# A step list for each engine in the banded mixer, two score buffers in turn, and merged up-products in the perceptrons of a six-layer transformer on one Trainium2 core

## The reference, cut to what matters

```python
def swa_sink_attention(h, w_in, b_in, sinks, w_out, cos, sin):   # 16 query heads, 2 key heads, head size 64
    qkv = h @ w_in + b_in
    q, k, v = jnp.split(qkv, [SWA_HEADS * D, (SWA_HEADS + KV) * D], axis=-1)
    q = apply_partial_rope(q.reshape(B, S, SWA_HEADS, D), cos, sin) * (D ** -0.5)
    k = apply_partial_rope(k.reshape(B, S, KV, D), cos, sin)
    ...
    s = jnp.where(mask, s, -jnp.inf)              # window of 128 keys back, causal
    m = jnp.maximum(jnp.max(s, axis=-1, keepdims=True), sink)
    e = jnp.exp(s - m)
    p = e / (jnp.sum(e, axis=-1, keepdims=True) + jnp.exp(sink - m))
    return (p @ v2).reshape(B, S, SWA_HEADS * D) @ w_out

def sqrelu_mlp(h, w_up, w_down):                  # 1024 -> 4096 -> 1024
    a = jnp.maximum(h @ w_up, 0)
    return (a * a) @ w_down
```

## Time and profile before

| | |
|---|---|
| runs (3) | 1585.6, 1586.77, 1589.15 us; median 1586.77 |
| profiled execution | 1580.09 us, span 1578.1 us, mean granted TensorE clock 0.974 |
| TensorE busy | 1483.8 us, 94% of the span |
| VectorE, ScalarE busy | 935.8 us (59%), 807.1 us (51%) |
| DMA | 242.24 MB, mean 153 GB/s |
| chain that ended last | TensorE 82%, ScalarE 8%, VectorE 6%, DMA 3% |

### The profile page before, as it was taken

The page is one execution under the profiler, slowest core; times in us unless marked ns, Lnnn a source line. Parts: engine busy times, 40 slices in busy tenths (PEclk is TensorE's granted clock), DMA queues, the critical chain, the costliest instruction groups (busy, mean ns, idle before and its releaser), DMA issues.

```text
span 1578.1 us, 20946 instructions
## 1 busy us (share of the span) xinstructions
PE 1483.8 (94%) x8815; PEld 1291.9 (82%) x8815; DVE 935.8 (59%) x1292; ACT 807.1 (51%) x1251; POOL 39.3 (2%) x72
## 2 busy tenths in 40 slices
PE   7988999999999999888999999989999899889988
PEld 5777999978889998766899987768999778777877
DVE  6673555465745455555455456645455479868984
ACT  6584444454534344433444436765344357756783
POOL 3000000000000000000000000000000010101010
PEclk8999999999999999999999999989999989989998
DMA  8432454544235454511354556324454534425430
GB/s 281 157 110 107 166 208 172 202 160 161 107 116 204 170 203 151 196 54 54 117 204 177 197 175 203 122 101 161 166 208 172 201 103 161 146 81 164 166 108 27
DMA packets 119465, 242.24 MB, mean 153 GB/s; under 512 B 3042, under 2 KB 48908, under 8 KB 119372
## 3 DMA queue, kind: packets, MB, share of 16 engines
q1 hardware_dynamic: 117616, 237.25, 42.5%
q0 software_dynamic: 1408, 3.52, 1.0%
q10 hardware_dynamic: 348, 0.13, 0.0%
HBM read 239.84 MB, written 1.05 MB: 153 GB/s over the span
## 4 chain that ended last, share of the span: by engine, by line
PE 82%; ACT 8%; DVE 6%; DMA 3%; issue 1%; POOL 0%; SPq 0%; DVEq 0%; POOLq 0%; ACTq 0%
PE pair L1092 24%; PE pair L1094 24%; PE pair L1093 23%; PE pair L1295 3%; PE pair L1246 2%; PE pair L1186 2%; DVE wlo L1553 2%; ACT sm L762 1%; ACT whi L656 1%; PE pair L1272 1%; ACT xhi L688 1%; PE pair L1241 1%; DVE xlo L1590 1%; DMA raw<-in_diff_w_out 1%; DMA raw<-in_w_in 1%
## 5 line engine op out<-in xcount | busy, mean ns | idle before, releaser
L1553 DVE TENSOR_TENSOR wlo<-raw,whi 128x2048 fp32r<-128x2048 f32 (+2 forms) x240 | 504.9, 2141 | 76.1 <-ACT whi L656 74.2
L656 ACT ACTIVATE whi<-raw 128x2048 fp32r<-128x2048 f32 (+2 forms) x240 | 416.5, 1782 | 103.8 <-DMA raw<-in_mlp_w_down 46.3
L1092 PE MATMUL pair<-xhi,whi 128*128 128x256 f32 x1024 | 291.0, 284 | 6.9 <-DVE xlo L1590 6.9
L1094 PE MATMUL pair<-xhi,wlo 128*128 128x256 f32 x1024 | 289.7, 283 | 0.0
L1093 PE MATMUL pair<-xlo,whi 128*128 128x256 f32 x1024 | 289.7, 283 | 0.0
L1092 PE MATMUL pair<-whi,xhi 128*128 128x512 f32 (+2 forms) x656 | 261.6, 399 | 22.7 <-DVE wlo L1553 13.3
L1094 PE MATMUL pair<-whi,xlo 128*128 128x512 f32 (+2 forms) x656 | 253.1, 386 | 0.0
L1093 PE MATMUL pair<-wlo,xhi 128*128 128x512 f32 (+2 forms) x656 | 252.8, 385 | 0.0
L1092 PE MATMUL pair<-whi,ahi 128*128 128x512 f32 x608 | 242.0, 398 | 5.6 <-DVE alo L1590 5.6
L1093 PE MATMUL pair<-wlo,ahi 128*128 128x512 f32 x608 | 239.1, 393 | 0.0
L1094 PE MATMUL pair<-whi,alo 128*128 128x512 f32 x608 | 238.9, 393 | 0.0
(11 more groups left out here) (248 smaller groups left out, 1465.5 us busy)
## 6 DMA issues: line engine op xcount, KB each, us to landing
raw<-in_mlp_w_up SPq DMA_DIRECT2D x32, 2048.0 KB, 8.6
raw<-in_mlp_w_down SPq DMA_DIRECT2D x32, 2048.0 KB, 7.5
raw<-in_diff_w_in SPq DMA_DIRECT2D x22, 1024.0 KB, 7.2
raw<-in_w_in SPq DMA_DIRECT2D x10, 2048.0 KB, 8.1
raw<-in_moba_w_in SPq DMA_DIRECT2D x12, 1024.0 KB, 6.2
raw<-in_diff_w_out SPq DMA_DIRECT2D x4, 2048.0 KB, 7.9
raw<-in_w_uq SPq DMA_DIRECT2D x4, 1152.0 KB, 5.4
raw<-in_moba_w_out SPq DMA_DIRECT2D x2, 2048.0 KB, 8.3
```

The source lines that it names most:

```text
L656: act.activation(whi[:, s, cols], raw[:, s, cols], ACT.Copy).then_inc(*t["hi_split"].one())
L1092: pe.matmul(dst, x_hi, w_hi, start=first, stop=False)
L1094: return pe.matmul(dst, x_lo, w_hi, start=False, stop=last)
L1553: dve.tensor_tensor(wlo[:, s, cols], raw[:, s, cols], whi[:, s, cols].bitcast(FP32), ALU.subtract)\
```

## The change

1. The banded mixer gets a list for each engine (`swa_tensor_steps`, `swa_scalar_steps`, `swa_vector_steps`) and its own reader `mix_swa` on each engine, with `BankUses` over `swa_bank_uses`. Head pairs use PSUM pair 0 and pair 3 in turn (`score_pair`). The first input block is queries 0 to 511, then keys and values, then the other queries. Queries are transposed for two head pairs at a time, into four half-pairs. The copy to `pT` moves from VectorE to ScalarE. The outputs' features go to `ahi_tiles` and `alo_tiles` instead of `xhi` and `xlo`. The first output block takes its units by columns, the second by features.
2. `keep_busy` is removed.
3. `xhi` and `xlo` are neighbours in one tile, `xparts`. A unit of an up block becomes one matmul of 512 columns (weights hi by both parts of x) and one of 256 (weights lo by x hi), so 64 matmuls a block instead of 96. Each bank holds one hidden tile: 256 columns of the large sum and 256 of the small. An up block uses both pairs 0 and 1. In each half ScalarE copies the small sums, VectorE adds the large ones from PSUM and frees the pair, VectorE takes relu times itself in one operation, ScalarE rounds, VectorE subtracts. A half starts when its two hidden tiles are done, the first one in the middle of the block.

```diff
+def swa_bank_uses():
+    scores = [[f"{what}{hp}" for hp in range(j, HEAD_PAIRS, 2) for what in ("scores", "turn")] for j in range(2)]
+    uses = {2: ["in2"], 3: ["in1"] + scores[1], 0: scores[0], 6: ["heads2"], 7: ["heads3"], 8: ["keys0"]}
+    for j in range(2):
+        uses[4 + j] = [f"heads{j}"] + [f"{what}{q}" for q in (j, 2 + j) for what in ("outputs", "features")]
+    return uses
...
-        xhi = sb("xhi", [P, KT, SEQ], FP32R)
-        xlo = sb("xlo", [P, KT, SEQ], FP32R)
+        xparts = sb("xparts", [P, 2, KT, SEQ], FP32R)
+        xhi, xlo = xparts[:, 0, :, :], xparts[:, 1, :, :]
...
-                return [(1024, 256), (0, BANK), (BANK, BANK)]
+                return [(0, BANK), (1024, 256), (BANK, BANK)]
...
+            steps = part("in", 0, 0, 8) + part("in", 1, 0, 7) + [("heads", 0)] + part("in", 1, 7, 8) + [("heads", 1)]
+            steps += part("in", 2, 0, 3) + [("keys", 0)] + part("in", 2, 3, 5) + [("scores", 0), ("scores", 1)]
+            steps += part("in", 2, 5, 8) + [("turn", 0), ("turn", 1), ("scores", 2), ("mix", 0), ("scores", 3), ("heads", 2)]
+            steps += [("heads", 3), ("mix", 1), ("turn", 2), ("features", 0), ("turn", 3), ("scores", 4)]
+            steps += [("mix", 2), ("scores", 5), ("mix", 3), ("turn", 4), ("features", 1), ("turn", 5)]
+            steps += [("scores", 6), ("mix", 4), ("scores", 7)] + part("out", 0, 0, 3) + [("mix", 5), ("turn", 7), ("turn", 6)]
+            steps += part("out", 0, 3, 4) + [("features", 2), ("mix", 6), ("mix", 7)] + part("out", 0, 4, 7) + [("features", 3)]
+            steps += part("out", 0, 7, 8) + part("out", 1, 0, 8)
...
+            steps = [("in_results", 0), ("in_results", 1), ("in_results", 2), ("split", 0), ("split", 1), ("heads", 0)]
+            steps += [("heads", 1), ("split", 0), ("split", 1), ("keys", 0), ("split", 0), ("split", 1)]
+            steps += [("scores", 0), ("scores", 1), ("outputs", 0), ("turn", 0), ("turn", 1), ("scores", 2)]
...
+            steps = [("split", 0), ("split", 1), ("in_results", 0), ("rope", 0), ("in_results", 1), ("heads", 0)]
+            steps += [("heads", 1), ("rope", 1), ("split", 0), ("keys", 0), ("split", 1), ("scores", 0)]
+            steps += [("scores", 1), ("split", 0), ("in_results", 2), ("rope", 2), ("scores", 2), ("scores", 3)]
...
-            return 0
+            return 3 * (hp % 2) if mixer == "swa" else 0
...
-                    used()
-                    act.activation(relu_at[b], pair[b][:, :, :].rearrange("p b n -> p (b n)"), ACT.Relu)\
-                        .then_inc(*t.emptied[b].one())
-                    act.wait_ge(*t.emptied[b].now())
-                    act.activation(ahi[:, b, :, :].rearrange("p f n -> p (f n)"), relu_at[b], ACT.Square)\
-                        .then_inc(*t["ahi_written"].one())
+                    for part in range(2):
+                        used(1)
+                        act.activation(rising(part), pair[part][:, :, SEQ:2 * SEQ], ACT.Copy).then_inc(*t["small_copied"].one())
+                        t.emptied[part].n += 1
+                    for part in range(2):
+                        act.wait_ge(*t["squared"].after())
+                        act.activation(risen_to(ahi, j % 2, part), risen(part), ACT.Copy).then_inc(*t["ahi_written"].one())
...
-                    free(j % 2)
...
-                        m = products(pair_tile(j % 2, f), (w_hi[:, k, cols], w_lo[:, k, cols]),
-                                     (xhi[:, k, :], xlo[:, k, :]), k == 0, k == KT - 1)
-                        if f % 2 and k == KT - 1:
+                        if k == 0 and f // 2 == 0:
+                            free(f % 2)
+                        cols, sums = slice(f * P, (f + 1) * P), pair[f % 2][:, f // 2, :]
+                        pe.matmul(sums, w_hi[:, k, cols], xparts[:, :, k, :], start=k == 0, stop=False)
+                        m = pe.matmul(sums[:, 0:SEQ], w_lo[:, k, cols], xhi[:, k, :], start=False, stop=k == KT - 1)
+                        if f // 2 and k == KT - 1:
...
+                    for part in range(2):
+                        used(1)
+                        dve.wait_ge(*t["small_copied"].after())
+                        dve.tensor_tensor(rising(part), pair[part][:, :, 0:SEQ], rising(part), ALU.add)\
+                            .then_inc(*t.emptied[part].one())
+                        dve.wait_ge(*t.emptied[part].now())
+                        dve.scalar_tensor_tensor(out=risen(part), in0=rising(part), scalar=0.0, in1=rising(part), op0=ALU.max,
+                                                 op1=ALU.mult).then_inc(*t["squared"].one())
+                    for part in range(2):
+                        dve.wait_ge(*t["squared"].now(1 - part))
+                        dve.wait_ge(*t["ahi_written"].after())
+                        dve.tensor_tensor(risen_to(alo, j % 2, part), risen(part), risen_to(ahi, j % 2, part).bitcast(FP32),
+                                          ALU.subtract).then_inc(*t["alo_written"].one())
```

More of the change, by code:

```diff
@@ new lines, in swa_tensor_steps, with part @@
+        def swa_tensor_steps():
+            def part(what, b, first, last):
+                return [(what, b, e) for e in range(first, last)]
+            steps = part("in", 0, 0, 8) + part("in", 1, 0, 7) + [("heads", 0)] + part("in", 1, 7, 8) + [("heads", 1)]
[6 more added lines that the diff above has]
+            steps += part("out", 0, 7, 8) + part("out", 1, 0, 8)
+            return steps
@@ L1633, in norm @@
                     split()
-            def biased_results(n):
-                c0, w = in_blocks("swa")[n]
-                p = 2 + n % 2
-                for tt in range(TT):
-                    used(1)
-                    m = dve.scalar_tensor_tensor(out=qkv[:, tt, c0:c0 + w], in0=pair[p][:, tt, 0:w], scalar=rstd[:, tt:tt + 1],
-                                                 in1=swab[:, c0:c0 + w], op0=ALU.mult, op1=ALU.add)
-                m.then_inc(*t.emptied[p].one())
             def rope(view, n, half, tables, place):
@@ L1822, in mix_tokens, with biased_results, rotated_keys @@
                         split((n,))
+            def biased_results(n, done):
+                c0, w = in_blocks("swa")[n]
+                for tt in range(TT):
+                    used(1)
+                    m = dve.scalar_tensor_tensor(out=qkv[:, tt, c0:c0 + w], in0=pair[2 + n % 2][:, tt, 0:w],
+                                                 scalar=rstd[:, tt:tt + 1], in1=swab[:, c0:c0 + w], op0=ALU.mult, op1=ALU.add)
+                m.then_inc(*done)
+            def rotated_keys():
+                chain(rotate_heads(D, 2))
+                k = qkv[:, :, 1024:1152].rearrange("p t (g d) -> p t g d", g=2)
+                both = qkv[:, :, 1280:1536].rearrange("p t (g r d) -> p t g r d", g=2, r=2)
+                for r in range(2):
+                    m = dve.tensor_copy(both[:, :, :, r, :], k)
+                return m
```

245 lines of the change are left out of this document (172 added, 73 removed).

## The result

| | before | after |
|---|---|---|
| median of the runs | 1587.96 us (1585.6 to 1591.03, 4 runs) | 1539.4 us (1537.26 to 1541.15, 4 runs) |
| ratio after / before | | 0.9686, 95% interval 0.9664 to 0.9707 |
| span, granted clock | 1578.1 us, 0.974 | 1539.4 us, 0.974 |

The change is 3% faster; 1544 was forecast. The page of the changed kernel, part 1 (beside the earlier trace rows): TensorE has 1088 instructions fewer and is busy 22.6 us less, though the span is 38.7 us shorter. The other 16.1 us were idle time. VectorE's busy time grew by 44.0 us, where about 40 were forecast.

What follows compares the result with a forecast made beforehand. TensorE, busy 94% of the span, bounds the kernel; the banded mixer has slack. Merge 13.5 plus mixer 29 is 42.5 us off 1580.1, giving 1537.6, with 6.7 us for the median 1544; forecast 1538 to 1550, range 1532 to 1560.

Steps and rivals of the forecast that it cites:

- the 79.2 us of work: Banded mixer, first input product to closing residual transposes: TensorE's summed work after the change at full clock, against 118.4 us before.
- 3 for handovers: Banded mixer: some 0.1 us for each handover that the listed durations leave out, 3 us added in all.
- The wait at heads 0: Banded mixer, before the first queries' transposes: TensorE newly waits 2.5 us for VectorE's split, bias and turning.
- the idle time in the attention: Banded mixer's attention without filler until scores 7: idle bits of 0.4 to 1.0 us, together 4 us.
- the walk: Banded mixer: the four lists stepped through with the durations, giving 7 us idle and about 4 us a pair.
- The tight place (3): Banded mixer: ScalarE's output-block splits precede the first exponentials, which end at 674; TensorE is covered until 674.4, under 1 us.
- my three conditions for being wrong: Merged matmul over 0.235 us, TensorE idle in the perceptrons, or granted clock below 0.8 in the attention stretch.
- my upper bound: Perceptron up blocks: a merged product at twice the pace of 256 columns, 0.2398 us, where nothing is gained.
- Rival 3: Perceptrons: merge fails, by two chunks at two matmuls' pace or the page's 2.5 ns; 11 to 13.5 us less, chance 0.07.
- cover: Perceptrons: time between wlo being ready and the next up block that reads it, 2.2 us before, 1.4 after.
- rival 4: Perceptrons: the split of the block after next makes TensorE wait; 4 us more gives 73 us lost, 1617; chance 0.02.
- that offset: Whole kernel: the median of the runs lies 6.7 us above the profiled execution, added to 1537.6 to expect 1544.

Runs made afterwards that it cites:

- the run with the early turn: Changed kernel with VectorE's bias and turning of the first query block moved between the two splits of weight block 2: 1536.67 us, ratio 0.9693 to before.
- The late split: Changed kernel with four extra chained ScalarE copies of 1024 elements before the splits in each up block's evacuation: 1660.85 us, ratio 1.0462 to before.
- the repeat: The changed kernel run again unchanged, on the chip of the three kernels beside it: 1542.52 us, ratio 0.9730 to before.

## Why the prediction was right, and where it was not

**The banded mixer: right, and a little better.** Forecast 89.2 us, measured 85.5, just under the named 86 to 93. To the 79.2 us of work the prediction added 7 us of idle time and 3 for handovers; the measured surplus over the same work is 6.3. The wait at heads 0 was sized rightly (2.5 us, measured 2.1), the idle time in the attention was not: 4 us, and the waits show 0.8. The clock was taken as full, and it was, but for the 2.7 us behind heads 0, which the walk did not have; they are worth about 1.7 us (3.8 less 2.1 in the run with the early turn), and two other executions did not have them. The rest, 85.5 less 79.2, 2.9 and 1.7, is 1.7 us that no row names; the 3 us for handovers can be at most that. So the idle time and the handovers were put too high and the half clock was left out, and that part of these cancels is luck. The tight place (3) held as forecast, covered by the input products, though what released it was another engine: ScalarE's splits were done at 671.13, exponentials 0 started at 672.20, when VectorE's `snk` was ready, and turn 0 followed at 675.93 without a wait of TensorE.

**Which part of it carried the gain.** Putting the scores on one pair costs 24.8 us in the mixer part. The order of the input blocks gives 7.1 us when it is made alone. These two make up 31.9 of the 32.9 us, though they were measured on different kernels, each in a single profile, and need not add. The prediction gave the wait for `wlo` and the slow start behind it no sum of its own.

**The perceptrons: the term that was mis-sized.** "It saves 13.4 ns in each of 1024 units, 13.7 us; I take 13.5": measured 6.7 ns in most units, 1024 x 6.7 ns = 6.9 us, by the marks 1.3 to 1.8 in each of four. One of my three conditions for being wrong, a merged matmul of over 0.235 us, was met: from a merged product to the next small one pass 0.240 us, and 0.113 from that to the next merged one (means over the block shown). It is the number of my upper bound, a merged product at the pace of two of 256 columns, but not its reason, since the operand in one piece ran no faster. I had added the paces of two streams that are each of one width. In a stream of both, the sum holds only in one of two states. Rival 3 had part of the size right and both of its causes wrong. The page "TensorE: Matmul & The Clock Gate" of the Trainium skill, section "Back-to-back issue gap", gives 2.5 ns a matmul beyond the columns, for matmuls taken singly, 2.6 us here; the measured 6.7 ns lies between it and the 13.4 of the homogeneous streams, and by the page alone the gain would have been missed by more than half.

**The evacuation: right.** 2.9 us from the block's end to the split, cover 1.63 us for 1.4, no wait of an up block for `wlo`, VectorE 44.0 us busier for about 40. The late split shows that the cover was real and how close: 4.32 us more on ScalarE cost 118 us. My price for rival 4 (73 us for 4 us more, which is 82 for 4.32) counted the waits alone, and they are 80 us; the half clock that they bring is another 39. The count of blocks was off: 24 wait, not 28, and the weight blocks behind them wait too.

**The clock: right.** With one pair it is 0.84 and value products take 2.83 us, with two it is 1.00 in the attention. In the kernel before, taking out the filler leaves 0.86 where 0.93 and 0.89 were granted with it. The page "TensorE: Matmul & The Clock Gate" of the Trainium skill, section "Part 1: The HAM clock gate", says that the throttled state is the default and that activity releases it; the trace agrees in direction. But the total does not move when the filler goes (0.9992 to 1.0025).

**The total.** Mixer 3.7 us better than forecast, merge 6.7 worse; by these the profiled execution should have been 1540.6, and it was 1541.15. That the sum came out so near is partly luck, as one term was too low and the other too high. The median was 1539.4 and not 6.7 us above the profile: that offset was a property of one execution of before and not of the kernels. It goes with the granted clock. Of the 56 runs of before beside the experiments, the shortest took 1581.25 us at a mean granted clock of 0.975, the longest 1593.51 at 0.963, and the others lie about a line between them, some 1 us for 0.001; the profile of before had 0.974. The changed kernel's four runs had 0.974, in the profiled one, and 0.977 to 0.979; in the repeat they had 0.970 to 0.977, and the median was 1542.52. At 0.977 both comparisons have a run of 1539.5 and 1539.91. So the 4.6 us between 1544 and the first median are no more than the clock's scatter between runs, and what sets that scatter was not found; whether the clock is its cause or goes along with one was not tested.

## What to carry to other kernels

When a chain score, exponential, transpose, value product holds TensorE at 40% of its time, give two of them a PSUM area each before anything else: lists for each engine without it lost 25 of the 33 us here. Price a merge of matmuls from a stream with the same mix of widths, not from the sum of two streams of one width each. And before a stretch is padded to hold the clock, fill the gaps with the other chain's work; then see which engine's list has a large operation ahead of a small one that TensorE waits for, as moving two steps ahead of one such operation gave 2.2 to 3.8 us in that stage.

## What was not expected of the hardware

- Alternating products of 512 and 256 columns have two paces at full clock: 0.3533 us and 0.3467 us a unit, 848 and 832 cycles of 2.4 GHz for 768 columns. Each lasts to the end of a block. All 24 up blocks that follow a down block without a stop have the upper one in both executions of the changed kernel. In opening pairs, which reach full clock from half clock, both occur, also for the same pair in two executions (third perceptron: 23.95 and 23.61 us from first to last). In the run with the late split, up blocks after a stop show both too. What picks the state was not found.
- The layout of the moving operand (two chunks of 256 or one of 512) made no difference: 0.353 us a unit both ways.
- A stop of 2.1 to 2.8 us on TensorE can cost more than itself, and does not always: behind the stop of 2.1 us at heads 0 the products ran at half clock until 663.03 in one execution and at full clock in another with the same list, which makes the stop's price 3.8 or 2.2 us.
- The second block's time differs by up to 11.6 us between executions (314.4 to 326.0) with the same instructions, with granted clocks of 0.95 to 0.91, so that the total of one profile can't settle a few us.
